# A two-block transformer kernel on one core: the attention probabilities of the first block are turned by VectorE and DMAs instead of TensorE

## What is computed

```python
s_s = jnp.einsum('btgrd,bgtkld->bgrtkl', qblk, ksel).astype(jnp.float32) * scale + b_s
p_s = masked_softmax(s_s.reshape(B, G, R, Q_BLOCK, -1), (d_s >= 0).reshape(B, G, 1, Q_BLOCK, -1)).reshape(shp)
o_s = jnp.einsum('bgrtkl,bgtkld->btgrd', p_s.astype(vsel.dtype), vsel)
s_w = jnp.einsum('btgrd,bsgd->bgrts', qblk, kw).astype(jnp.float32) * scale + rel_bias_heads(d_w, rel_table)
p_w = masked_softmax(s_w, m_w)
o_w = jnp.einsum('bgrts,bsgd->btgrd', p_w.astype(vw.dtype), vw)
o = g[..., 0:1] * o_cmp + g[..., 1:2] * o_slc + g[..., 2:3] * o_win
```

## Time and profile before

| | us |
|---|---|
| median of 3 runs (2205.61 to 2206.26) | 2205.96 |
| the profiled execution | 2205.11 |
| its span, from the first to the last instruction | 2203.3 |
| TensorE busy in it | 2188.5 (99%) |
| VectorE busy | 1327.7 (60%) |
| ScalarE busy | 1045.9 (47%) |
| GpSimd busy | 164.1 (7%) |

### The profile page before, as it was taken

One profiled execution on the slowest core, in us unless ns is written; L12 is line 12 of the kernel. 1 busy time (PEld: TensorE's weight loads), 2 busy tenths in 40 slices (PEclk: granted clock), 3 DMA queues, 4 the chain that ended last, 5 costly groups with the idle time before them and its releaser, 6 DMA issues.

```text
span 2203.3 us, 26723 instructions
## 1 busy us (share of the span) xinstructions
PE 2188.5 (99%) x10087; PEld 1818.1 (83%) x10087; DVE 1327.7 (60%) x1632; ACT 1045.9 (47%) x1313; POOL 164.1 (7%) x278
## 2 busy tenths in 40 slices
PE   9999999999999999999999999999999999999998
PEld 7888888888888888888888888888888888888886
DVE  6655665555555555455556776577666666765546
ACT  6555564444444444444444455355454444544333
POOL 1000000000000000010001344000000000000000
PEclk9999999999999999999999999999999999999999
DMA  9544457667666766677766667757775666656753
GB/s 334 193 132 146 149 174 267 209 184 227 204 206 188 229 200 200 202 226 225 224 198 210 191 195 218 266 181 231 209 210 176 205 189 205 206 173 199 258 202 113
DMA packets 367909, 449.05 MB, mean 204 GB/s; under 512 B 148305, under 2 KB 183281, under 8 KB 366672
## 3 DMA queue, kind: packets, MB, share of 16 engines
q1 hardware_dynamic: 354272, 412.87, 59.4%
q0 software_dynamic: 13264, 34.76, 5.1%
q10 hardware_dynamic: 288, 0.27, 0.0%
HBM read 415.32 MB, written 8.39 MB: 192 GB/s over the span
## 4 chain that ended last, share of the span: by engine, by line
PE 94%; DVE 3%; ACT 2%; DMA 1%; issue 1%; SPq 0%; POOL 0%; ACTq 0%; DVEq 0%; POOLq 0%
PE bank L402 29%; PE bank L404 29%; PE bank L403 29%; DVE wlo L382 1%; PE bank L416 1%; ACT whi L375 1%; PE bank L418 1%; PE bank L417 1%; PE bank L2045 0%; PE bank L435 0%; PE bank L2274 0%; DMA xT<-in_x_t 0%; PE bank L2261 0%; PE bank L2371 0%; PE bank L2370 0%
## 5 line engine op out<-in xcount | busy, mean ns | idle before, releaser
L382 DVE TENSOR_TENSOR wlo<-raw,whi 128x1024 fp32r<-128x1024 f32 x749 | 904.0, 1216 | 719.0 <-ACT whi L375 716.7
L375 ACT ACTIVATE whi<-raw 128x1024 fp32r<-128x1024 f32 x749 | 780.7, 1054 | 765.2 <-PE bank L404 749.9
L402 PE MATMUL bank<-whi,T1H 128*128 128x512 f32 (+1 forms) x2100 | 822.9, 392 | 1.2 <-DVE wlo L382 1.1
L404 PE MATMUL bank<-whi,T1L 128*128 128x512 f32 (+1 forms) x2100 | 814.7, 388 | 0.0
L403 PE MATMUL bank<-wlo,T1H 128*128 128x512 f32 (+1 forms) x2100 | 814.4, 388 | 0.0
L402 PEld LDWEIGHTS bank<-whi,T1H 128*128 128x128 f32 x2100 | 394.4, 188 | 83.3 <-DVE wlo L382 3.7
L404 PEld LDWEIGHTS bank<-whi,T1L 128*128 128x128 f32 x2100 | 394.1, 188 | 81.7
L403 PEld LDWEIGHTS bank<-wlo,T1H 128*128 128x128 f32 x2100 | 394.4, 188 | 78.8
L402 PE MATMUL bank<-whi,T2bH 128*128 128x512 f32 x352 | 136.9, 389 | 0.0
L403 PE MATMUL bank<-wlo,T2bH 128*128 128x512 f32 x352 | 136.9, 389 | 0.0
L404 PE MATMUL bank<-whi,T2bL 128*128 128x512 f32 x352 | 136.9, 389 | 0.0
(11 more groups left out here) (397 smaller groups left out, 1806.7 us busy)
## 6 DMA issues: line engine op xcount, KB each, us to landing
raw<-in_ret_w_in SPq DMA_DIRECT2D x64, 1024.0 KB, 5.5
raw<-in_w_ffn_gate SPq DMA_DIRECT2D x44, 1024.0 KB, 5.2
raw<-in_w_ffn_up SPq DMA_DIRECT2D x44, 1024.0 KB, 5.7
raw<-in_w_ffn_down SPq DMA_DIRECT2D x44, 1024.0 KB, 5.2
raw<-in_attn_w_in SPq DMA_DIRECT2D x40, 1024.0 KB, 5.4
raw<-in_w_in SPq DMA_DIRECT2D x39, 1024.0 KB, 5.1
raw<-in_ret_w_in SPq DMA_DIRECT2D x64, 512.0 KB, 4.6
raw<-in_ret_w_out SPq DMA_DIRECT2D x32, 1024.0 KB, 5.1
```

The costliest lines, as they stand in the source:

```text
L375: eng.activation(hi_[:, s, :, :n], raw[:, c % RAWS, HALF * hf:HALF * (hf + 1), :n], ACT.Copy).then_inc(hi_ready, 1)
L382: eng.tensor_tensor(lo[:, s, :, :n], raw[:, c % RAWS, HALF * hf:HALF * (hf + 1), :n], hi_[:, s, :, :n].bitcast(F32), ALU.subtract).then_in ...
L402: eng.matmul(o, TH[:, kt, xs], hi_[:, s, t, :n], start=first and t == 0, stop=False)
L404: m = eng.matmul(o, TL[:, kt, xs], hi_[:, s, t, :n], start=False, stop=last and t == HALF - 1)
```

## The change

`prob_T` and ScalarE's copies out of bank 6 are gone. For each head VectorE runs one `transpose` of 768 columns from `PB` into a new tile `PS` (`nsa_squares(h)`, step U0+2h+4, ahead of that step's `split_lo`). For each pair of heads SyncE and GpSimd start eight DMAs each that carry the squares of `PS` to `PT` (`pair_across`), SyncE's behind the load of chunks 27, 29, 31 and 33. `scores` of both units of a head go into one visit (steps 41, 43, ... 55), and so do VectorE's maxima and ScalarE's exponentials of both (steps 43, 45, ... 57) and VectorE's scaling of both (steps 44, 46, ... 58). `values` of two heads go into one visit, in steps 51, 55, 59 and 63. Later pieces shift by two steps, one `mix_norm` by eight; tiles are placed anew; the load of `gB` moves behind the convolution's copies. The hunks that only rename semaphore counts of the second block, declare semaphores or place one tile anew are left out.

```diff
@@ -139,10 +139,11 @@
-    PT = at("PT", PJ + 20 * KB, [P, 2, 2, 384])
+    PT = [at("PT0", R0 + 8 * KB, [P, 2, 2, 384]), at("PT1", PJ + 20 * KB, [P, 2, 2, 384])]
...
-    PB = at("PB", MS + 20 * KB, [P, 2, 2, 384])
-    dqZ = [at("dqZ0", R0, [P, 4, T]), at("dqZ1", MS + 28 * KB + 512, [P, 4, T])]
+    PB = at("PB", MS, [P, 2, 2, 384])
+    PS = [at("PS0", MS + 23 * KB, [P, 2, 2, 384]), at("PS1", MS + 17 * KB, [P, 2, 2, 384])]
+    dqZ = [at("dqZ0", R0, [P, 4, T]), at("dqZ1", R0 + 16 * KB, [P, 4, T])]
@@ -543,7 +544,7 @@
-    CONV = 66
+    CONV = 68
@@ -571,6 +572,16 @@
+
+    def pair_across(eng, g, rows_, done):
+
+        eng.wait_ge(p_sq, 2 * g + 2)
+        if g:
+            eng.wait_ge(done, g * (ACROSS // 2))
+        if g >= 2:
+            eng.wait_ge(nsa_pv, 2 * g - 2)
+        for r in rows_:
+            group_across(eng, line4(PS[g % 2]), line4(PT[g % 2]), r, done)
 
@@ -593,6 +604,9 @@
+            for g in range(NH // 2):
+                if c == (U0 + 4 * g + 6 + 7) // 2:
+                    pair_across(sp, g, (0, 1), p_in)
@@ -686,7 +700,6 @@
-        pool.dma_start(gB[:, :], spread(A["group_gain"], D)).then_inc(gg_in, 16)
@@ -699,6 +712,8 @@
+        for g in range(NH // 2):
+            pair_across(pool, g, (2, 3), p_in2)
@@ -709,6 +724,7 @@
+        pool.dma_start(gB[:, :], spread(A["group_gain"], D)).then_inc(gg_in, 16)
@@ -902,17 +918,12 @@
             for n in range(2):
-                if p == U0 + 8 * n + 14:
+                if p == U0 + 8 * n + 16:
                     act.wait_ge(nsa_pv, 4 * n + 4)
                     head_evac(Aq, n, nsa_o)
-            u = p - U0 - 5
-            if 0 <= u < NU:
-                act.wait_ge(p_T, u + 1)
-                if u >= 4:
-                    act.wait_ge(nsa_pv, u // 2 - 1)
-                act.activation(PT[:, u // 2 % 2, u % 2, :], bank[6][:, 0:384], ACT.Copy).then_inc(pT_out, 1)
-            u = p - U0 - 2
-            if 0 <= u < NU:
+            for u in range(NU):
+                if p != U0 + u // 2 * 2 + 2:
+                    continue
                 act.wait_ge(s_max, u + 1)
@@ -929,6 +940,7 @@
+                        act.wait_ge(nsa_pv, 6)
@@ -947,19 +959,19 @@
-            if p == U0 + 23:
+            if p == U0 + 25:
...
-            if p == U0 + 25:
+            if p == U0 + 27:
...
-            if p == 79:
+            if p == 81:
...
-            if p == 82:
+            if p == 84:
@@ -1391,11 +1403,10 @@
 
-            u = p - U0 - 2
-            if 0 <= u < NU:
+            for u in range(NU):
+                if p != U0 + u // 2 * 2 + 2:
+                    continue
                 dve.wait_ge(s_full, u + 1)
-                if u >= 4:
-                    dve.wait_ge(p_T, u - 3)
                 c, pb = 2 * (u % 4), PB[:, u // 2 % 2, u % 2, :]
@@ -1403,8 +1414,9 @@
                 ts(nmx[:, c:c + 2], nmx[:, c:c + 2], -1.0, None, MUL).then_inc(s_max, 1)
-            u = p - U0 - 3
-            if 0 <= u < NU:
+            for u in range(NU):
+                if p != U0 + u // 2 * 2 + 3:
+                    continue
                 c = 2 * (u % 4)
@@ -1427,9 +1439,9 @@
-            if p == U0 + 24:
+            if p == U0 + 26:
...
-            if p == U0 + 26:
+            if p == U0 + 34:
@@ -1454,9 +1466,9 @@
-            if p == 81:
+            if p == 83:
...
-            if p == 83:
+            if p == 85:
@@ -1470,6 +1482,15 @@
 
+        def nsa_squares(h):
+            g = h // 2
+            dve.wait_ge(p_norm, 4 * h + 4)
+            if g >= 2 and h % 2 == 0:
+                dve.wait_ge(p_in, (g - 1) * (ACROSS // 2))
+                dve.wait_ge(p_in2, (g - 1) * (ACROSS // 2))
+            dve.transpose(PS[g % 2][:, h % 2, :, :].rearrange("p k s -> p (k s)"),
+                          PB[:, h % 2, :, :].rearrange("p k s -> p (k s)")).then_inc(p_sq, 1)
+
@@ -1497,6 +1518,9 @@
                 p = 8 * b + h
+                for n in range(NH):
+                    if p == U0 + 2 * n + 4:
+                        nsa_squares(n)
                 if p < QUARTERED:
@@ -2023,17 +2047,11 @@
 
-        def prob_T(u):
-            pe.wait_ge(p_norm, 2 * u + 2)
-            if u:
-                pe.wait_ge(pT_out, u)
-            for n in range(3):
-                m = pe.transpose(bank[6][:, n * P:(n + 1) * P], PB[:, u // 2 % 2, u % 2, n * P:(n + 1) * P], ident)
-            m.then_inc(p_T, 1)
-
...
             g = h // 4
-            pe.wait_ge(pT_out, 2 * h + 2)
+            if h % 2 == 0:
+                pe.wait_ge(p_in, (h // 2 + 1) * (ACROSS // 2))
+                pe.wait_ge(p_in2, (h // 2 + 1) * (ACROSS // 2))
             if h == 4:
@@ -2042,7 +2060,7 @@
                         n, v = j + s, (Akv[:, s, 6 * HD:8 * HD], Akw[:, s, 2 * HD:4 * HD])[kind]
-                        m = mm(o, PT[:, h % 2, kind, n * P:(n + 1) * P], v[:, g * HD:(g + 1) * HD], start=False,
+                        m = mm(o, PT[h // 2 % 2][:, h % 2, kind, n * P:(n + 1) * P], v[:, g * HD:(g + 1) * HD], start=False,
                                stop=kind == 1 and s == j)
@@ -2052,8 +2070,6 @@
-            if k == 2:
-                pe.wait_ge(pT_out, NU)
@@ -2141,12 +2157,11 @@
                 pe.wait_ge(pcT_out, 4)
-            if 0 <= p - U0 < NU:
-                scores(p - U0)
-            if 0 <= p - U0 - 3 < NU:
-                prob_T(p - U0 - 3)
+            for u in range(NU):
+                if p == U0 + u // 2 * 2:
+                    scores(u)
             for h in range(NH):
-                if p == U0 + 2 * h + 6:
+                if p == U0 + h // 2 * 4 + 10:
                     values(h)
```

More of the change, by code:

```diff
@@ L160, in two_blocks @@
     z1 = at("z1", PJ + 4 * KB, [P, J, W])
-    z2 = at("z2", R0 + 16 * KB, [P, J, W])
+    z2 = at("z2", MS + 18 * KB, [P, J, W])
     cwB = at("cwB", MS + 8 * KB, [P, 3, W])
@@ L294, in two_blocks @@
         sem(x) for x in ("cs_full", "cs_sub", "cs_exp", "pc_ready", "pc_T", "pcT_out"))
-    gexp, s_full, s_max, s_exp, p_norm, p_T, pT_out, nsa_pv, nsa_o = (
-        sem(x) for x in ("gexp", "s_full", "s_max", "s_exp", "p_norm", "p_T", "pT_out", "nsa_pv", "nsa_o"))
+    gexp, s_full, s_max, s_exp, p_norm, nsa_pv, nsa_o = (
+        sem(x) for x in ("gexp", "s_full", "s_max", "s_exp", "p_norm", "nsa_pv", "nsa_o"))
     d_T, dT_out, z_full, d_log, d_sp, d_arg, d_cap, d_a, d_pv, d_o = (
@@ L612, in probs_across @@
         def probs_across(k):
-            sp.wait_ge(p_sq, 2 * k + 2)
+            sp.wait_ge(p_sq, NH + 2 * k + 2)
             if k >= 2:
@@ L758, in _ @@
             if what == "p":
-                pool.wait_ge(p_sq, 2 * k + 2)
+                pool.wait_ge(p_sq, NH + 2 * k + 2)
                 if k >= 2:
@@ L1072, in exps @@
             if u >= 2:
-                act.wait_ge(p_sq, u - 1)
+                act.wait_ge(p_sq, NH + u - 1)
             if u >= 4:
@@ L2264, in in2_at @@
                         if a % 2 == 0:
-                            pe.wait_ge(p_in, (u // 2 + 1) * (ACROSS // 2))
-                            pe.wait_ge(p_in2, (u // 2 + 1) * (ACROSS // 2))
+                            pe.wait_ge(p_in, (NH // 2 + u // 2 + 1) * (ACROSS // 2))
+                            pe.wait_ge(p_in2, (NH // 2 + u // 2 + 1) * (ACROSS // 2))
                         if u == 0:
```

## The result

| | before | changed |
|---|---|---|
| median of 15 runs each, us | 2205.67 | 2209.61 |
| lowest to highest | 2205.36 to 2207.64 | 2208.80 to 2212.04 |
| profiled execution, its span | 2203.3 | 2207.3 |

The ratio of the times is 1.0018, with a 95% interval of 1.0011 to 1.0025: 3.9 us slower. That is just under the 0.2% that I had set as the bound of "same", though the interval leaves out 1. The forecast was 2208.5, and +3.2 us against the kernel before.

The account below looks back on a forecast made before the run. In the first attention a VectorE-ScalarE loop of 8.71 us a head was to outlast TensorE's work; half 59 at 199.8 and two heads' values left until visit 63 gave net +3.2 us, 2208.5 us, range 2206.3 to 2211.8.

Parts of the forecast that it names:

- What bounds the stage: First attention, between 134 and 200: TensorE waits some 9 us for `wlo`, and the VectorE-ScalarE loop sets the time.
- The loop: Steps 45 to 59: `split_lo`, maxima, exponentials, `split_hi`, `split_lo`, scaling, transpose; 8.71 us a head against 7.98 before.
- the one term without a row: VectorE's transpose of 768 columns, estimated from instructions of 512 and 1024 columns at 0.89 us, bounds 0.63 and 1.26.
- What lengthens the loop: On VectorE, scaling now follows the exponentials and the transpose stands between two `split_lo`s; 8.71 against 7.98 us a head.
- The end of the attention: TensorE's half 59 starts at 199.8, half 62 at 213.2, half 64 near 223.
- TensorE's own earliest start of half 59: TensorE without waits from half 44 at 134.2, its halves, scores and values summed, reaches 190.6.
- the 0.1 of a half behind a visit: On TensorE, a half right after a visit takes 2.85 us instead of 2.74, already inside the 0.66 for scores.
- The sum: Whole program: net +3.2 us, 2208.3 from the profiled execution or 2209.2 from the median; 2208.5 taken.
- The turns: Sixteen turns taken off TensorE in the first attention, 0.33 us each, 5.3 us in all.
- The rival in which TensorE stays the bound: With a loop of 7.4 us or less a head, TensorE never waits; 2199.0 us, chance 0.06.
- What was costed at nothing: ScalarE's lost copies, SyncE's DMAs, squares landing (7.9 us a pair), convolution copies (0.9 us in hand), `head_evac`, later shifts: no cost.
- The rule of the skill: Turn 128x128 on TensorE; VectorE's blocks at 311 ns would make the loop 9.68 us and the time 2215.

Follow-up runs that it names:

- exps_late: The changed kernel with ScalarE's exponentials of a head moved behind the even `split_hi`; 2200.31 us, ratio 0.9976 to the kernel before.
- joined_only: The kernel before with scores, maxima, exponentials and scaling of a head's two units joined, turns still on TensorE; 2206.18 us, ratio 1.0002.
- scaling_late: The changed kernel with VectorE's transpose and the scaling of a head both moved behind the next head's maxima; 2200.27 us, ratio 0.9977 to the kernel before.

## Why the prediction was right

- **What bounds the stage.** Right. TensorE waits for `wlo` there, and for nothing else. It was to be some 9 us. The list has 10.9, and by the starts half 59 is 8.9 us later than in exps_late, where TensorE hardly waits.
- **The loop.** 8.71 us a head was worked out and 8.71 measured. The transpose, the one term without a row, was taken at 0.89 between bounds of 0.63 and 1.26, and took 0.90. Its price by columns, taken between two sizes of instruction, came out to 0.01.
- **What lengthens the loop.** Only half right. The prediction names two things, the scaling behind the exponentials and the transpose. But its own sum without the transpose is 8.71 - 0.89 = 7.82, under the 7.98 of before, and joined_only, with the scaling in that place, has 7.71. Against the kernel before, the transpose alone makes the loop longer. The scaling does lie in the loop, as scaling_late shows with its 3.6 us, but the joining takes one wait for ScalarE out of it, and that outweighs the scaling.
- **The end of the attention.** Half 59 was put at 199.8 and started at 199.85, half 62 at 213.2 and 213.38, half 64 near 223 and at 223.05. TensorE's own earliest start of half 59, put at 190.6, is seen in exps_late, at 190.94. The sum behind it counts the 0.1 of a half behind a visit twice, in the 0.66 of the scores and in the 41.7, 0.6 us in all; it has 56.4 from half 44 on, and exps_late has 56.6 with 0.4 of waiting in it, so the slip did no harm.
- **The sum.** +3.2 worked out, +3.9 between the medians. The lag at step 83 is 3.5; the other 0.4 comes in later parts that the change doesn't touch and is within what executions differ by. The time is only 0.5 us under the 0.2% line, so that it fell on the side of "same" is partly luck. The mechanism is not. By its own terms the lower end of the range is 2208.3 - 1.8 = 2206.5, not 2206.3, which changes nothing here.
- **The turns.** Priced at 5.3 us of TensorE. The kernels in which TensorE hardly waits are 5.5 under the kernel before. The rival in which TensorE stays the bound had 6.1, with the waits of the first steps gone too. At the first transposes of the second block exps_late is 5.6 ahead of the kernel before (1196.5 against 1202.1), and it still waits 0.4 ahead of half 45, so that price was nearly right. At the end of the profiled executions the lead is 4.9, between the medians 5.5; the profiled execution of the kernel before is itself 0.6 under its median. How much of the 5.5 the turns bring and how much the later exponentials was not run, as no kernel has the exponentials late and the turns on TensorE. But in the kernel before TensorE's listed waits for `wlo` in this stage are 0.6 us, so later exponentials alone could give back little more than that.
- **What was costed at nothing.** Right in the outcome, off in one size. The copies of the convolution cost nothing: issued from 224.8 to 226.9, they were used at 234.3. `head_evac` started at 190.34, and behind it ScalarE still idled 0.94 us before the exponentials at 191.88. But issue and landing of a pair's squares were put at 7.9 us from the earlier trace rows and took about 12, see below.
- **The rule of the skill.** The Trainium skill, "VectorE: DVE Perf Modes", section "Rules for kernel authors", prefers TensorE for turning 128x128. In the changed kernel that held; it did not hold for the stage as such, since exps_late turns on VectorE and is 5.5 us faster than the kernel that turns on TensorE. Where the transpose stands decided it.

## What to carry to other kernels

Low busy shares do not show room: here VectorE at 58% and ScalarE at 57% could take no 0.9 us more in one place and took it free in another. Write down the loop of waits between two in-order engines with start-to-start distances, compare its length with the bound engine's work of the same steps, and take the maximum step by step, since what TensorE waits early is not given back later. When an engine's work is to grow, first look in which idle time of that engine it can stand; and before giving up on a change that loses a little, look for the instruction ahead of which the other engine's next stage is queued: one number made this one as fast as the fastest here.

## What was not expected

A pair's sixteen DMAs took longer than in the second block. Issues of the changed kernel (KB each, median us to landing), and SyncE's first eight:

```profile
PT<-PS POOLq DMA_DIRECT2D x32, 48.0 KB, 5.4
PT<-PS SPq DMA_DIRECT2D x32, 48.0 KB, 5.3
```

```profile
148.00 6.92 SPq L457 DMA_DIRECT2D PT<-PS  x8
```

With 1.5 times the bytes and pieces of the earlier trace rows the landing took twice as long and the issue 1.3 times. The DMA share of 150 to 202 is 0.66, where the earlier trace rows had 0.39 in about the same steps. By these figures (an estimate) the squares of pair 0 were there at about 148.0 + 6.9 + 5.3 = 160.2; the first product that reads them starts at 169.4, so that 9 us were left and not 14. In exps_late the stage is shorter, and they still never show as a wait of TensorE. Why the landing took longer is not shown. How much sooner `values` could ask for them was not tried, nor was a kernel without the DMAs.
